# The LRU's gate products taken from high and low parts, in three products instead of one in full precision

## The chip, the cores and the metric

The kernel runs on one core of a Trainium2 chip. The metric is the device time of one execution in microseconds (us), taken as the median of several runs. The engines are named as the profile names them: PE multiplies matrices, PEld loads its weights, DVE and ACT do elementwise work, POOL does little here, and SP issues the transfers between the memory of the device and the core.

## The reference

One layer of a streaming encoder trunk is computed for 512 prompt positions and 8 x 16 sample positions, which makes T = 640 rows of width 1024. After a norm, one wide product with `w_in` feeds three branches: an attention with a forget gate (FoX), a gated linear recurrence (RG-LRU), and gated linear attention (GLA). Their outputs are merged by gates, and an MLP follows. The change touches only the LRU branch:

```python
xc, conv_new = causal_conv(lx, conv_buf, p['lru_conv_w'], p['lru_conv_b'])
hseq, h_last = rg_lru(xc, h0, p['lru_w_a'], p['lru_b_a'], p['lru_w_x'], p['lru_b_x'], p['lru_lambda'])
y_lru = jax.nn.gelu(lg) * hseq.astype(x.dtype)

def rg_lru(x, h0, w_a, b_a, w_x, b_x, lam):
    xb = x.reshape(B, T, LRU_BLOCKS, LRU_BLOCK_DIM)        # 8 blocks of 128 columns
    r = sigmoid(einsum('btni,nij->btnj', xb, w_a) + b_a)   # gate product 1
    i = sigmoid(einsum('btni,nij->btnj', xb, w_x) + b_x)   # gate product 2
    log_a = LRU_C * r * log_sigmoid(lam)
    a = exp(log_a); mult = sqrt(-expm1(2.0 * log_a))
    u = mult * i * x                                       # then h[t] = a[t] * h[t-1] + u[t]
```

## The kernel before, in words

All large products are made from high and low parts. A weight block of 128 output columns (512 KB) is loaded to `w_raw`, ACT casts it to its high part (`hi`, line L1115), DVE subtracts that from the raw block to give the low part (`lo`, line L1541), and PE runs, for each half of the 640 columns and each of 8 slices, three products: high by high, high by low, low by high (`block`, line L584). That is 24 matmuls of 320 columns for a half, 48 for a block. Two sets of buffers alternate, and the two halves have a PSUM bank each (`Z[0]`, `Z[1]`).

The LRU stage works through 8 blocks of 128 channels. The program calls `lru_window(n, ...)` for n = 0 to 8 on every engine; each engine runs its own list of instructions in the order written, and semaphores tie the lists together. Window n does two things at once. For channel block n (`cur`) it computes the two projections: `lx` goes to the tile `XP` (ACT lines L1280, L1299, L1300), is convolved by DVE (L1777 to L1791) into `XC`, and `lg` goes to `LG` (L1120) and into the GELU. For channel block n-1 (`lag`) it makes the gates and the recurrence. The windows 1 to 7 do both; window 0 has only `cur`, window 8 only `lag`. In window n the lists are, in order:

- PE: the first half of the `lx` block, the gate products of block n-1 (`lru_gates`, L790), the second half of the `lx` block, both halves of the `lg` block.
- ACT: copy of the first half of `lx` (L1280), tanh of the GELU (L1285), four tanhs on the gate products (L1290), one more tanh (L1296), copies of the second half of `lx` (L1299, L1300), `hi` of the next window's `lx` block (L1115), exp and square of the decay (L1305, L1306), first half of `lg` (L1120), square root (L1313), second half of `lg` (L1120), square for the GELU (L1318), `hi` of the next window's `lg` block (L1115), and, after DVE's output, the cast to `YH` (L1322).
- DVE: L1762, L1766, `lo` (L1541), L1771 (waits for ACT's L1306), the convolution (it waits for ACT's copies of both halves), L1794, the small fixes L1798 to L1800, the scan over 640 steps (L1801), the output product (L1802, which releases L1322), L1808 (waits for L1318), `lo` (L1541), L1813.
- SP: for window n two weight blocks, and then, when the gate products of the window before are done (`g_mm`), the two 128x128 gate weights into `WG` (L478). A transfer that waits holds all the later ones in SP's list.

The gate products of the kernel before are plain f32 matmuls of `WG` with `XC`, four instructions of 320 columns for each block. The profile shows such an instruction as two records. Their semaphores are `xc_ready` (convolution done), `wg_in` (gate weights arrived) and `r_act` (ACT has read the gates of the block before). Most of the tiles named here are pieces of one large buffer, so that rows call them `arena`.

Of the kernel before, what the change touches and what calls it, by code (L numbers as in the profile page):

```python
# [18 lines left out]
ALU = mybir.AluOpType  # L19
ACT = mybir.ActivationFunctionType  # L20
AX = mybir.AxisListType
F32 = mybir.dt.float32
F32R = mybir.dt.float32r
BF16 = mybir.dt.bfloat16

P = 128
NEG = -1.0e30
ARENA = 22600
# [66 lines left out]
def build(nc, ins, outs):  # L95
# [5 lines left out]
    TP, D = x_prompt.shape[1], x_prompt.shape[2]  # L101
    NB, TS_ = x_sample.shape[0], x_sample.shape[1]
    T = TP + NB * TS_
    HT = T // 2
# [46 lines left out]
    with ExitStack() as ctx:  # L151
# [8 lines left out]
        bank = [psum[:, i, :] for i in range(8)]  # L160
# [33 lines left out]
        arena_at = nc.sbuf_base - 4 * ARENA  # L194
# [20 lines left out]
        A0 = KT * T  # L215
# [6 lines left out]
        def sems(names):  # L222
            return [sem(n) for n in names.split()]
# [23 lines left out]

        wg_in, xc_ready, g_mm, rx_act, r_act, a_act, m_dve, m_act, h_ready, yl_hi, yl_done = sems(
            "wg_in xc_ready g_mm rx_act r_act a_act m_dve m_act h_ready yl_hi yl_done")
        ge_sq, ge_dve, ge_act, ge_out, last_dve, last_pe, last_sb = sems(  # L250
            "ge_sq ge_dve ge_act ge_out last_dve last_pe last_sb")

# [29 lines left out]
        XPW = CONV_W - 1 + TP + NB * (CONV_W - 1 + TS_)  # L282
        (WG, LG, GQ, TG, Y2, RA, RX, AA, TH, A2, MM, UU, HH, XC, XP, LS) = carve(
            A0, (2, P), (T,), (T,), (T,), (T,), (T,), (T,), (T,), (T,), (T,), (T,), (T,), (T,), (T,), (XPW + 1,), (D,))
        XPS = XP[:, CONV_W - 1 + TP:XPW].rearrange("p (b t) -> p b t", b=NB)

        (QG, KG, KTl, ZG, BC, E1, E2, E3, KEM, VT2, VN, QGB, S0, SA, OS, RG, GU, SG) = carve(
            A0, (T,), (T,), (T,), (T,), (T,), (T,), (T,), (T,), (2, P), (2, T), (NT, GLA_DV),
# [69 lines left out]
        def _(sp):  # L358
# [110 lines left out]
            def lru_loads(n, first=False):  # L469
                b = n * 2 + B_LRU  # L470
                c = (lambda c0: n.ds(P, P, c0) if n.terms else slice(c0 + n.c * P, c0 + (n.c + 1) * P))
                load(b, B_LRU % 2, w_in_v[:, :, c(clx)])
                load(b + 1, 1 - B_LRU % 2, w_in_v[:, :, c(clg)])
                if not first:
                    sp.wait_ge(g_mm, n.v)
                nd = n.ds() if n.terms else slice(n.c, n.c + 1)
                for i, w in enumerate((lru_wa, lru_wx)):
                    sp.dma_start(WG[:, i, :], w[0, nd].rearrange("n i j -> (n i) j")).then_inc(wg_in, 16)  # L478
# [93 lines left out]
        def _(pe):  # L572
# [34 lines left out]
            for k in range(KT):  # L607
                mm = pe.transpose(bank[6][:, k * NR:(k + 1) * NR], vrow[0:NR, k * P:(k + 1) * P], idf[0:NR, 0:NR])
# [4 lines left out]
            for r in range(16):  # L613
                mm = pe.transpose(bank[2 + r // 4][0:FOX_HEADS, (r % 4) * P:(r % 4 + 1) * P],
                                  cp_raw[:, r * FOX_HEADS:(r + 1) * FOX_HEADS], idf[:, :])
# [5 lines left out]
            for t in range(NT):  # L621
                mm = pe.transpose(bank[6][:, t * 8:t * 8 + 8], lfT[0:FOX_HEADS, tok(t)], idf[0:FOX_HEADS, 0:FOX_HEADS])
# [3 lines left out]
            for t in range(NT):  # L626
                mm = pe.transpose(bank[7][:, t * 8:t * 8 + 8], cT[0:FOX_HEADS, tok(t)], idf[0:FOX_HEADS, 0:FOX_HEADS])
# [153 lines left out]


            def lru_gates(n):
                pe.wait_ge(xc_ready, (n + 1).v)
                pe.wait_ge(wg_in, (n * 32 + 32).v)
                if n.terms or n.c > 0:
                    pe.wait_ge(r_act, n.v)
                for i in range(2):
                    for h in range(2):
                        mm = pe.matmul(bank[2 + 2 * i + h][:, 0:HT], WG[:, i, :], XC[:, h * HT:(h + 1) * HT],  # L790
                                       start=True, stop=True)
                mm.then_inc(g_mm, 1)

            def lru_window(n, lag):
# [10 lines left out]
            for n in range(LRU_N):  # L805
                mm = pe.transpose(bank[2 + n // 4][0:36, (n % 4) * P:(n % 4 + 1) * P], last[:, n, :], idf[:, :])
# [141 lines left out]
            for c in range(NKC):  # L948
# [3 lines left out]
                for t in range(NT):  # L952
                    mm = rows_block(bank[PAIR[t]], c * KC_W, t, WHW, WLW, b % 2, c == 0, c == NKC - 1)
# [149 lines left out]
        def _(act):  # L1103
            step = Steps(act, act_step)

            def hi(b, s):

                if b.terms or b.c >= 2:
                    act.wait_ge(z_done[1], (b + -1).v)
                hi_to(b, s, WH[s][:, :, :], raw[s][:, :, :])  # L1110
# [158 lines left out]
            def lru_window(n, cur, lag):  # L1269

                b = n * 2 + B_LRU
                s = B_LRU % 2
                m = n + -1
                if not lag:
                    hi(b + 1, 1 - s)
                if cur:
                    if lag:
                        act.wait_ge(xc_ready, n.v)
                    act.wait_ge(z_done[0], (b + 1).v)
                    act.copy(XP[:, 3:3 + HT], Z[0][:, 0:HT]).then_inc(z_free[0], 1)  # L1280
                else:
                    gate(1, Lin(0), b, 0, 0)
                if lag:
                    act.wait_ge(ge_dve, n.v)
                    act.activation(TG[:, :], GQ[:, :], ACT.Tanh, scale=GELU_A).then_inc(ge_act, 1)  # L1285
                    act.wait_ge(g_mm, n.v)
                    act.wait_ge(lru_cols, 1)
                    for dst, bk, r, done in ((RX, 4, R_BX, rx_act), (RA, 2, R_BA, r_act)):
                        for h in range(2):
                            ins_ = act.activation(dst[:, h * HT:(h + 1) * HT], bank[bk + h][:, 0:HT], ACT.Tanh, scale=0.5,  # L1290
                                                  bias=one(col[:, at(m), r:r + 1]))
                        ins_.then_inc(done, 1)
                    act.wait_ge(r_act, n.v)

                    c4, c4n = one(lru_c4[:, 0:1, at(m)]), one(lru_c4[:, 1:2, at(m)])
                    act.activation(TH[:, :], RA[:, :], ACT.Tanh, scale=c4n, bias=c4n)  # L1296
                if cur:
                    act.wait_ge(z_done[1], (b + 1).v)
                    act.copy(XP[:, 3 + HT:3 + TP], Z[1][:, 0:TP - HT])  # L1299
                    act.copy(XPS[:, :, CONV_W - 1:], Z[1][:, TP - HT:HT].rearrange("p (b t) -> p b t", t=TS_)).then_inc(z_free[1], 1)  # L1300
                else:
                    gate(1, Lin(0), b, 0, 1)
                hi(b + 2, s)
                if lag:
                    step(act.activation(AA[:, :], RA[:, :], ACT.Exp, scale=c4, bias=c4))  # L1305
                    act.activation(A2[:, :], AA[:, :], ACT.Square).then_inc(a_act, 1)  # L1306
                if cur:
                    if lag:
                        act.wait_ge(ge_out, n.v)
                    evac(b + 1, 0, LG[:, 0:HT])  # L1310
                if lag:
                    act.wait_ge(m_dve, n.v)
                    act.activation(MM[:, :], MM[:, :], ACT.Sqrt).then_inc(m_act, 1)  # L1313
                if cur:
                    evac(b + 1, 1, LG[:, HT:T])
                    for h in range(2):
                        act.wait_ge(z_free[h], (b + 2).v)
                    act.activation(GQ[:, :], LG[:, :], ACT.Square, scale=GELU_B ** 0.5).then_inc(ge_sq, 1)  # L1318
                    hi(b + 3, 1 - s)
                if lag:  # L1320
                    act.wait_ge(h_ready, n.v)
                    act.copy(YH[:, at(m), :], MM[:, :].unsqueeze(1)).then_inc(yl_hi, 1)  # L1322
# [208 lines left out]
        def _(dve):  # L1531
# [221 lines left out]
            def lru_window(n, cur, lag):  # L1753
# [19 lines left out]
                if cur:  # L1773
# [4 lines left out]
                    for j in range(CONV_W):  # L1778
                        w = one(col[:, at(n), R_CW + j:R_CW + j + 1])
# [12 lines left out]
                if lag:  # L1792
                    dve.wait_ge(m_act, n.v)
                    step(dve.scalar_tensor_tensor(out=UU[:, :], in0=UU[:, :], scalar=0.5, in1=MM[:, :], op0=ALU.mult, op1=ALU.mult))  # L1794

                    h0 = col[:, at(m), R_H0:R_H0 + NB].rearrange("p a b -> p (a b)").unsqueeze(2)
                    first_a, first_u = by_sample(AA)[:, :, 0:1], by_sample(UU)[:, :, 0:1]
                    step(dve.tensor_tensor(fix[:, :, :], first_a, h0, ALU.mult))  # L1798
                    step(dve.tensor_tensor(first_u, first_u, fix[:, :, :], ALU.add))
                    step(dve.memset(first_a, 0.0))  # L1800
                    step(dve.tensor_tensor_scan(HH[:, :], AA[:, :], UU[:, :], 0.0, ALU.mult, ALU.add))  # L1801
                    dve.scalar_tensor_tensor(out=MM[:, :], in0=Y2[:, :], scalar=0.5, in1=HH[:, :], op0=ALU.mult,  # L1802
                                             op1=ALU.mult).then_inc(h_ready, 1)
                    dve.tensor_copy(last[:, at(m), 27:28], HH[:, TP - 1:TP].unsqueeze(1))
                    step(dve.tensor_copy(last[:, at(m), 28:36], by_sample(HH)[:, :, TS_ - 1:TS_].rearrange("p b o -> p o b")))
# [248 lines left out]
```

## Time and profile before

| what | value |
|---|---|
| median of the runs | 1556.79 us |
| lowest and highest of 3 | 1556.17 and 1559.05 us |
| the profiled execution: its own time | 1559.7 us |
| the profiled execution: span of its trace | 1558.0 us |
| granted TensorE clock, mean over the span | 0.989 |
| PE, PEld, DVE, ACT busy | 97%, 90%, 44%, 39% of the span |

The span reaches from the first to the last recorded instruction, and the execution's own time is 1.7 us longer. A granted clock of 1.00 is 2.4 GHz and 0.50 is 1.2 GHz. The busy share of PE is high because matmuls are pipelined and their records overlap; the pitch from one start to the next is a better measure of what a matmul costs in a stream.

### The profile page before, as it was taken

How to read it: one execution, taken by the hardware profiler on the slowest of the kernel's cores; microseconds unless marked ns; L12 is line 12 of the kernel's file. 1: busy time of each engine (PE TensorE's matmuls, PEld its weight loads, DVE VectorE, ACT ScalarE, POOL GpSimd, SP SyncE). 2: the span in 40 equal slices, each digit the busy share in tenths (PEclk: the TensorE clock that was granted, in tenths of full speed). 3: DMA queues.
4: the chain of work that ended last, by engine and by line, in shares of the span. 5: the costliest groups of instructions: out<-in, count | busy, mean ns of one | idle time of the engine just before them, and what ended most of it. 6: DMA issues, size and time to landing. Idle time of an engine off the chain costs nothing.

```text
span 1558.0 us, 25466 instructions
## 1 busy us (share of the span) xinstructions
PE 1509.3 (97%) x9798; PEld 1400.6 (90%) x9798; DVE 692.5 (44%) x1185; ACT 609.4 (39%) x1092; POOL 10.8 (1%) x25
## 2 busy tenths in 40 slices
PE   6999999999999989999999999999899999999997
PEld 6899999989999979998988989987898998998986
DVE  6455555532357872334554543345432323323235
ACT  6233333322157762224554541234441441431532
POOL 1000000000000000000000000000100000000000
PEclk9999999999999999999999999999899999999999
DMA  4645456332313222242332322333022222222221
GB/s 144 162 132 160 123 138 161 83 86 67 85 48 87 61 71 68 67 112 55 113 111 54 112 84 81 99 144 95 28 80 72 78 81 69 80 78 70 82 93 70
DMA packets 224956, 143.50 MB, mean 92 GB/s; under 512 B 7654, under 2 KB 211111, under 8 KB 224892
## 3 DMA queue, kind: packets, MB, share of 16 engines
q1 hardware_dynamic: 224900, 142.72, 31.9%
q8 instruction: 39, 0.64, 0.2%
q14 instruction: 17, 0.14, 0.0%
HBM read 129.86 MB, written 12.84 MB: 92 GB/s over the span
## 4 chain that ended last, share of the span: by engine, by line
PE 84%; DVE 7%; ACT 4%; issue 3%; DMA 2%; DVEq 0%; ACTq 0%; SPq 0%
PE psum L584 57%; PE psum L939 16%; PE psum L691 1%; PE psum L719 1%; PE psum L864 1%; DVE arena L1801 1%; ACT arena L1290 1%; DVE arena L1856 1%; PE psum L702 1%; PE psum L651 1%; PE psum L662 1%; ACT w_hi L1115 1%; PE psum L907 1%; PE psum L905 1%; PE psum L599 1%
## 5 line engine op out<-in xcount | busy, mean ns | idle before, releaser
L584 PE MATMUL psum<-XH,w_hi 128*128 128x320 f32 x1936 | 610.7, 315 | 5.4 <-DVE XL L1547 2.0
L584 PE MATMUL psum<-XH,w_lo 128*128 128x320 f32 x1936 | 600.6, 310 | 0.0
L584 PE MATMUL psum<-XL,w_hi 128*128 128x320 f32 x1936 | 600.6, 310 | 0.0
L1541 DVE TENSOR_TENSOR w_lo<-w_raw,w_hi 128x1024 fp32r<-128x1024 f32 x177 | 216.6, 1224 | 374.7 <-ACT w_hi L1115 374.1
L584 PEld LDWEIGHTS psum<-XH,w_hi 128*128 128x128 f32 x1936 | 365.9, 189 | 18.1 <-issue 7.4
L584 PEld LDWEIGHTS psum<-XL,w_hi 128*128 128x128 f32 x1936 | 366.0, 189 | 0.8
L584 PEld LDWEIGHTS psum<-XH,w_lo 128*128 128x128 f32 x1936 | 365.6, 189 | 0.0
L1115 ACT CAST w_hi<-w_raw 128x1024 fp32r<-128x1024 f32 x177 | 185.3, 1047 | 326.7 <-PE psum L939 155.3
L939 PE MATMUL psum<-w_hi,YH 128*128 128x512 f32 x320 | 125.4, 392 | 2.7 <-DVE YL L1936 2.7
L939 PE MATMUL psum<-w_hi,YL 128*128 128x512 f32 x320 | 125.0, 391 | 0.0
L939 PE MATMUL psum<-w_lo,YH 128*128 128x512 f32 x320 | 125.0, 391 | 0.0
L584 PE MATMUL psum<-YH,w_hi 128*128 128x320 f32 x384 | 119.6, 311 | 1.0 <-DVE YL L1672 1.0
L584 PE MATMUL psum<-YL,w_hi 128*128 128x320 f32 x384 | 119.3, 311 | 0.0
L584 PE MATMUL psum<-YH,w_lo 128*128 128x320 f32 x384 | 119.3, 311 | 0.0
L1970 DVE TENSOR_TENSOR YL<-arena,YH 128x320 f32 (+1 forms) x64 | 31.5, 493 | 148.7 <-ACT YH L1481 148.7
L1120 ACT ACTIVATE arena<-psum 128x320 f32<-128x320 f32 x96 | 41.5, 433 | 101.6 <-PE psum L584 101.4
L939 PEld LDWEIGHTS psum<-w_hi,YH 128*128 128x128 f32 x320 | 60.5, 189 | 15.5 <-issue 3.0
L584 PEld LDWEIGHTS psum<-YH,w_hi 128*128 128x128 f32 x384 | 72.8, 190 | 1.2 <-issue 1.1
L584 PEld LDWEIGHTS psum<-YL,w_hi 128*128 128x128 f32 x384 | 72.7, 189 | 0.0
L584 PEld LDWEIGHTS psum<-YH,w_lo 128*128 128x128 f32 x384 | 72.6, 189 | 0.0
L939 PEld LDWEIGHTS psum<-w_lo,YH 128*128 128x128 f32 x320 | 60.4, 189 | 12.6
L939 PEld LDWEIGHTS psum<-w_hi,YL 128*128 128x128 f32 x320 | 60.5, 189 | 12.4
(249 smaller groups left out, 1420.2 us busy)
## 6 DMA issues: line engine op xcount, KB each, us to landing
w_raw<-in_w_in_dram SPq DMA_DIRECT2D x88, 512.0 KB, 3.9
w_raw<-in_w_up_dram SPq DMA_DIRECT2D x32, 512.0 KB, 4.0
w_raw<-in_w_down_dram SPq DMA_DIRECT2D x32, 512.0 KB, 3.5
w_raw<-in_w_branch_dram SPq DMA_DIRECT2D x24, 512.0 KB, 3.9
arena<-in_cache_fox_k_dram SPq DMA_DIRECT2D x8, 1024.0 KB
arena<-in_cache_fox_v_dram SPq DMA_DIRECT2D x8, 1024.0 KB
out_dram<-arena SPq DMA_DIRECT2D x16, 256.0 KB, 2.4
arena<-in_state_gla_dram SPq DMA_DIRECT2D x4, 1024.0 KB, 5.4
```

Source lines behind the costliest of these rows:

```text
L584: mm = pe.matmul(Z[h][:, 0:HT], w[s][:, k, :], x[:, k, h * HT:(h + 1) * HT], start=(k == 0 and i == 0), stop=(k == KT - 1 and i == 2))
L599: mm = pe.transpose(bk[:, k * P:(k + 1) * P], HS[:, t % 2, (4 * q + k) * P:(4 * q + k + 1) * P], idf[:, :])
L651: mm = pe.transpose(TBK[j % 2][:, i * P:(i + 1) * P], KC[par][:, 4 * j + i, :], idf[:, :])
L662: mm = pe.transpose(TBK[j % 2][:, (i - 4 * j) * P:(i - 4 * j + 1) * P], src[:, par, tok(i % NT)], idf[:, :])
L691: pe.matmul(S[:, 0:w], QT[:, par, tok(t)], KTt[:, par, 0:w], start=True, stop=False)
L702: mm = pe.transpose(TBK[2][:, i * P:(i + 1) * P], SP[:, p % 2, i * P:(i + 1) * P], idf[:, :])
L719: mm = pe.matmul(O[:, 0:P], KVN[:, i, :], pt[:, i * P:(i + 1) * P], start=(i == 0), stop=(i == t))
L939: mm = pe.matmul(O[:, 0:HD], x[:, k0 + k, tok(t)], w[c][:, k, :], start=(first and k == 0 and i == 0), stop=(last and k == KC_W - 1 and i ...
L1115: act.copy(dst, src).then_inc(w_hi, 1)
L1120: act.activation(dst, Z[h][:, 0:HT], ACT.Copy, scale=scale).then_inc(z_free[h], 1)
L1541: dve.tensor_tensor(dst, src, h.bitcast(F32), ALU.subtract).then_inc(w_lo, 1)
L1970: dve.tensor_tensor(YL[:, bass.ds(j, 1), half], UQ[:, half].unsqueeze(1), YH[:, bass.ds(j, 1), half].bitcast(F32), ALU.subtract).then_inc( ...
```

## The change

The gate products are made the same way as the large ones. ACT casts the gate weights `WG` (256 columns) to `WGH` and the convolution output `XC` (640 columns) to `XGH`; DVE subtracts to get `WGL` and `XGL`; PE runs 12 matmuls of the fp32r type for a block instead of 4 of type f32. The two casts stand on ACT after L1318 and ahead of the `hi` of the next `lg` block. The two subtractions stand on DVE between L1794 and L1798. In window n they belong to channel block n, and PE uses them in window n+1. SP loads new gate weights when DVE's second subtraction is done (`xg_lo_done`), and no longer when the gate products are done. The four new tiles lie behind those of the stage in the same buffer.

```diff
 (SP, lru_loads)
                 if not first:
-                    sp.wait_ge(g_mm, n.v)
+                    sp.wait_ge(xg_lo_done, n.v)
                 ...
 (PE)
             def lru_gates(n):
-                pe.wait_ge(xc_ready, (n + 1).v)
-                pe.wait_ge(wg_in, (n * 32 + 32).v)
+                pe.wait_ge(xg_hi_done, (n + 1).v)
                 if n.terms or n.c > 0:
                     pe.wait_ge(r_act, n.v)
-                for i in range(2):
-                    for h in range(2):
-                        mm = pe.matmul(bank[2 + 2 * i + h][:, 0:HT], WG[:, i, :], XC[:, h * HT:(h + 1) * HT],
-                                       start=True, stop=True)
+                for j, (w, x) in enumerate(((WGH, XGH), (WGH, XGL), (WGL, XGH))):
+                    if j == 1:
+                        pe.wait_ge(xg_lo_done, (n + 1).v)
+                    for i in range(2):
+                        for h in range(2):
+                            mm = pe.matmul(bank[2 + 2 * i + h][:, 0:HT], w[:, i, :], x[:, h * HT:(h + 1) * HT],
+                                           start=(j == 0), stop=(j == 2))
                 mm.then_inc(g_mm, 1)
 (ACT, lru_window)
                     act.activation(GQ[:, :], LG[:, :], ACT.Square, scale=GELU_B ** 0.5).then_inc(ge_sq, 1)
+                    act.wait_ge(wg_in, (n * 32 + 32).v)
+                    act.copy(WGH[:, :, :], WG[:, :, :])
+                    act.wait_ge(xc_ready, (n + 1).v)
+                    act.copy(XGH[:, :], XC[:, :]).then_inc(xg_hi_done, 1)
                     hi(b + 3, 1 - s)
 (DVE, lru_window)
                 if lag:
                     dve.wait_ge(m_act, n.v)
                     step(dve.scalar_tensor_tensor(out=UU[:, :], in0=UU[:, :], scalar=0.5, in1=MM[:, :], op0=ALU.mult, op1=ALU.mult))
+                if cur:
+                    dve.wait_ge(xg_hi_done, (n + 1).v)
+                    dve.tensor_tensor(WGL[:, :, :], WG[:, :, :], WGH[:, :, :].bitcast(F32), ALU.subtract)
+                    dve.tensor_tensor(XGL[:, :], XC[:, :], XGH[:, :].bitcast(F32), ALU.subtract).then_inc(xg_lo_done, 1)
+                if lag:
                     h0 = col[:, at(m), R_H0:R_H0 + NB].rearrange("p a b -> p (a b)").unsqueeze(2)
```

The lines of the changed kernel are numbered higher, by 7 to 17 in the rows that follow. First the list of DVE in the body of the loop over the windows 1 to 7, from the end of the convolution to the scan. Before:

```order
L1791 COPY last<-arena 128x24
L1794 SCALAR_TENSOR_TENSOR arena<-arena 128x640
L83 REGISTER_ALU
L1798 ISA
L1798 TENSOR_TENSOR fix<-arena,col 128x8
```

And with the change, at the same place:

```order
L1804 COPY last<-arena 128x24
L1807 SCALAR_TENSOR_TENSOR arena<-arena 128x640
L83 REGISTER_ALU
L1809 REGISTER_ALU
L1810 TENSOR_TENSOR wg_lo<-arena,wg_hi 128x256
L1811 TENSOR_TENSOR xg_lo<-arena,xg_hi 128x640
L1815 ISA
L1815 TENSOR_TENSOR fix<-arena,col 128x8
```

The two subtractions came in ahead of the fixes, and so ahead of the scan and of the output product behind them. Next ACT's list from the copy of the second half of `lg` to the cast to `YH`, before:

```order
L1120 ACTIVATE arena<-psum 128x320
L1318 ACTIVATE arena<-arena 128x640
L1114 REGISTER_ALU
L1115 CAST w_hi<-w_raw 128x1024
L1322 ISA
L1322 COPY YH<-arena 128x640
```

And with the change:

```order
L1129 ACTIVATE arena<-psum 128x320
L1327 ACTIVATE arena<-arena 128x640
L1328 ISA
L1329 CAST wg_hi<-arena 128x256
L1330 REGISTER_ALU
L1331 CAST xg_hi<-arena 128x640
L1123 REGISTER_ALU
L1124 CAST w_hi<-w_raw 128x1024
L1335 ISA
L1335 COPY YH<-arena 128x640
```

The two casts stand between the GELU's square and the weight block's high part. The cast of the weight block now follows a wait for the convolution.

## Rows read from the trace of the kernel before

**Rows 1.** The page: the chain that ended last, shares by engine.

```profile
PE 84%; DVE 7%; ACT 4%; issue 3%; DMA 2%; DVEq 0%; ACTq 0%; SPq 0%
```

**Rows 2.** Chain that ended last, 425 to 590 us: start, us, what.

```profile
462.00 0.18 DVE fix L1798
...
496.50 0.18 DVE fix L1798
...
502.63 1.68 ACT arena L1290 x4
...
507.53 0.75 ACT arena L1306
...
513.75 0.18 DVE fix L1798
...
565.50 0.18 DVE fix L1798
```

**Rows 3.** Timeline of ACT, 494 to 520 us; in brackets the idle time before.

```profile
510.55 0.42 ACT L1120 ACTIVATE arena<-psum 128x320 f32<-128x320 f32 x1
511.06 0.74 ACT L1318 ACTIVATE arena<-arena 128x640 f32<-128x640 f32 x1
...
516.77 0.73 ACT L1322 CAST YH<-arena 128x640 f32 x1 [4.03 <-DVE arena L1802]
```

**Rows 4.** Timeline of DVE, 494 to 520 us.

```profile
512.69 0.17 DVE L1791 COPY last<-arena 128x24 f32 x1
512.77 0.82 DVE L1794 SCALAR_TENSOR_TENSOR arena<-arena 128x640 f32<-128x640 f32 x1
...
515.82 0.82 DVE L1802 SCALAR_TENSOR_TENSOR arena<-arena 128x640 f32<-128x640 f32 x1
...
517.65 1.22 DVE L1541 TENSOR_TENSOR w_lo<-w_raw,w_hi 128x1024 fp32r<-128x1024 f32 x1
518.79 0.82 DVE L1813 TENSOR_TENSOR YL<-arena,YH 128x640 f32 x1
```

**Rows 5.** Timeline of PE, 444 to 449 us: gate products between two halves.

```profile
443.82 0.31 PE L584 MATMUL psum<-XH,w_lo 128*128 128x320 f32 x1
...
446.17 2.31 PE L790 MATMUL psum<-arena 128*128 128x320 f32 x8
...
448.46 0.31 PE L584 MATMUL psum<-XL,w_hi 128*128 128x320 f32 x1
```

**Rows 6.** Timelines of ACT, then of SP, windows 0 and 1, 426 to 470 us.

```profile
443.38 0.74 ACT L1318 ACTIVATE arena<-arena 128x640 f32<-128x640 f32 x1
...
448.65 1.78 ACT L1290 ACTIVATE arena<-psum,col 128x320 f32<-128x320 f32 x4 [1.22 <-PE psum L790]
...
452.04 0.32 ACT L1299 COPY arena<-psum 128x192 f32<-128x192 f32 x1 [0.54 <-PE psum L584]
...
453.88 1.05 ACT L1115 CAST w_hi<-w_raw 128x1024 fp32r<-128x1024 f32 x1 [1.35 <-DMA w_raw<-in_w_in_dram]
...
459.07 0.44 ACT L1120 ACTIVATE arena<-psum 128x320 f32<-128x320 f32 x1 [0.18 <-PE psum L584]
...
448.65 0.35 SPq L478 DMA_DIRECT2D arena<-in_lru_w_a_dram  x1
...
450.02 1.02 SPq L363 DMA_DIRECT2D w_raw<-in_w_in_dram  x2
```

**Rows 7.** Timeline of PE: the first matmuls behind two long pauses.

```profile
42.61 0.47 PE L622 MATMUL psum<-ident,arena 8*128 8x8 f32 x5 [1.90 <-DVE arena L1601]
...
584.80 1.87 PE L806 MATMUL psum<-ident,last 128*36 128x128 f32 x8 [6.38 <-DVE fix L1821]
```

**Rows 8.** Stretches: us, busy PE, PEld, DVE, ACT, POOL, PEclk, DMA share, GB/s.

```profile
42.00:48.00 6.00, 5.39 (x28) 5.37 (x29) 4.40 (x7) 0.00 (x0) 0.00 (x0) 0.72 0.12 15
52.00:54.00 2.00, 0.93 (x9) 0.84 (x8) 1.33 (x2) 1.63 (x3) 0.00 (x0) 1.00 0.05 14
582.00:590.00 8.00, 5.20 (x22) 4.83 (x23) 3.12 (x7) 4.72 (x6) 0.00 (x0) 0.57 0.00 0
```

More of the change, by code:

```diff
@@ L249, in build @@
             "wg_in xc_ready g_mm rx_act r_act a_act m_dve m_act h_ready yl_hi yl_done")
+        xg_hi_done, xg_lo_done = sems("xg_hi_done xg_lo_done")
         ge_sq, ge_dve, ge_act, ge_out, last_dve, last_pe, last_sb = sems(
@@ L285, in build @@
         XPS = XP[:, CONV_W - 1 + TP:XPW].rearrange("p (b t) -> p b t", b=NB)
+        A_LG = -(-(A0 + 2 * P + 13 * T + XPW + 1 + D) // 8) * 8
+        XGH, XGL = (nc.alloc_sbuf_tensor_at(name, [P, T], F32R, offset=arena_at + 4 * (A_LG + i * T))
+                    for i, name in enumerate(("xg_hi", "xg_lo")))
+        WGH, WGL = (nc.alloc_sbuf_tensor_at(name, [P, 2, P], F32R, offset=arena_at + 4 * (A_LG + 2 * T + i * 2 * P))
+                    for i, name in enumerate(("wg_hi", "wg_lo")))
+        assert A_LG + 2 * T + 4 * P <= ARENA
         (QG, KG, KTl, ZG, BC, E1, E2, E3, KEM, VT2, VN, QGB, S0, SA, OS, RG, GU, SG) = carve(
```

## The prediction

> **What bounds the kernel now.** First I read the page's chain by engine: 84% of it is PE [rows 1], so one would expect any cheaper matmul to help. That is a mean over stages, so next I read the chain in the stretch that is changed, the LRU stage at about 425 to 590 us. There the chain hardly touches PE. It goes round once in each window: the fixes, scan and output product on DVE, then ACT's list with L1290 and L1306 in it, then DVE's convolution, L1794 and the fixes again [rows 2]. The same instruction, L1798, stands at 496.50 and at 513.75, so a turn is 17.25 us; from the first at 462.00 to the last shown at 565.50 there are six turns, and 103.50 / 6 is 17.25 too. ACT waits 4.03 us for DVE before L1322 [rows 3], and DVE waits for ACT elsewhere: the two pass one thread to and fro.
>
> Then I read what PE needs for a window. Sixteen starts from 443.82 to 446.17 give a pitch of 0.147 us for a matmul of 320 columns [rows 5]. The gate products begin at 446.17, and the second matmul behind them at 448.46, so that the first stood at 448.31 by the pitch: 2.14 us for the four f32 instructions. With 96 matmuls in two blocks PE needs 96 x 0.147 + 2.14 = 16.25 us in a turn of 17.25. PE idles 1.0 us in each turn, and the loop over ACT and DVE sets the pace.
>
> **What PE gains.** Twelve fp32r matmuls at that pitch take 1.76 us, 0.38 less than the 2.14. PE's need falls to 15.9 us. In the steady windows this is worth nothing, since PE already waits there; if PE did set the pace, it would be 8 x 0.38 = 3.0 us.
>
> **What ACT and DVE have to do more.** The trace of before has no cast or subtraction of 256 columns. For 640 columns a cast took 0.73 us (L1322) [rows 3] and one for 1024 columns 1.05 [rows 6], so a line through both gives 0.41 for 256. A subtraction took 0.82 for 640 columns (L1813) and 1.22 for 1024 (L1541) [rows 4], so 0.42 for 256. Bounds: not under nothing, not over the 0.73 and 0.82 of the wider ones; I take the lines, since the size lies near and the kind of work is the same. Back-to-back instructions overlap by 0.08 (L1791 starts at 512.69, lasts 0.17, and L1794 starts at 512.77; it has 0.09 there) [rows 4].
>
> **Where it stands in the loop.** In the frame of the turn that ends at 513.75:
> - ACT ends the copies and the square L1318 at 511.80 [rows 3]. The cast of the gate weights fits behind it, to 512.1, in a time in which ACT idled later. It costs nothing, covered by the 4.03 us.
> - The convolution is done at 512.69 + 0.17 = 512.86 [rows 4]. ACT picks such a signal up 0.13 later (L1802 ends at 515.82 + 0.82 = 516.64 [rows 4], L1322 starts at 516.77 [rows 3]) and casts 640 columns: 512.99 to 513.72.
> - DVE does L1794 meanwhile (512.77 to 513.59) and then waits for that cast. Its first subtraction starts at 513.76, almost exactly when L1798 started before. So the wait itself costs nothing over the 0.16 that DVE lost there anyway, and the subtractions cost all: (0.42 - 0.08) + (0.82 - 0.08) = 1.08. L1798 starts at 514.84 instead of 513.75: **1.09 us later**.
> - Behind it on DVE are queued the fixes, the scan, the output product, and for the product ACT waits with L1322; ACT's table load and L1280 follow at once, then all of the turn. Nothing in the turn has slack to take it up. A turn becomes 18.34 us.
>
> What is late next: the cast of the next `lg` block now follows the cast of `XC`, so it ends near 514.8 instead of 512.75. Its subtraction stood at 517.65 behind DVE's output product [rows 4] and moves on by 1.09 too, so it does not see this. On PE the first four gate matmuls wait for the cast, the other eight for the subtraction, and the second half of `lx` stands behind them. They end 8 x 0.147 = 1.2 us after the subtraction, that is about 1.3 us after L1798; ACT's L1290 wants them 502.63 - 496.50 = 6.1 us after it [rows 2]. The second half of `lx` is done 3.5 us later, at 4.8, and ACT wants it when L1290 has ended, at 7.8. PE has room. On SP the gate weights no longer wait for the gate products but for the second subtraction, which is earlier, and two weight loads stand behind them in the list; in the steady windows no cast waits for a load, so this brings nothing there.
>
> **Windows 0 and 1.** Window 0 has no recurrence on DVE, so its subtractions delay nothing: L1318 at 443.38 [rows 6], casts to 445.1, subtractions to 446.3, while PE reaches the gates at 446.17 and needs the low parts only at 446.76. Here PE and SP count. The gate products end 0.38 us earlier, so L1299, which waited for PE, goes from 452.04 to 451.66 [rows 6]. The gate weights are issued at 446.45 instead of 448.65, so the next weight load goes from 450.02 to 447.82 and lands by 451.7; its cast then follows L1299 after 0.35, at 452.0 instead of 453.88. That gives 1.87 us to the thread, and the convolution of window 1 ends at 459.24 instead of 461.11. But ACT cannot use all of it: its copy of the second half of `lg` waits for PE, and moves only from 459.07 to 458.69. Then come L1318 (0.51 behind, as in [rows 3]) at 459.20, the two casts from 459.84 to 460.9, and the two subtractions: L1798 at 462.03, against 462.00 before. So window 1 costs nothing: the gain of 1.87 pays for its 1.09 and for ACT's late casts.
>
> **Sum.** Windows 2 to 7 are six turns of 1.09 = 6.5 us, and with the 0.03 of window 1 it is +6.6 us. Window 8 has neither casts nor subtractions. The stages before and after are bound by PE as they were; they just begin later. Against the profiled execution's own 1559.7 us that gives 1566.3; that execution lies 2.9 us above the median, and I put the same 6.6 us on the median: **1563.4 us**, 0.42% slower. The case's own range: with the window 1 paying its 1.09 in full (its gain lost elsewhere) 7.6 us, and with no overlap at DVE (1.24 a turn, seven turns) 8.7; with a 256-column subtraction that costs nothing 6 x 0.74 = 4.4. So 1561.2 to 1565.5.
>
> **Rivals.**
> - *The work is hidden.* DVE is busy 44% of the span, so 1.1 us of it could vanish in idle time. If the thread did not run through L1798, only the gain of windows 0 and 1 would be left: 0 to -1.9 us, 1554.9 to 1556.8. Against it: DVE runs its list in order, the scan is in the thread in all seven turns, and the 0.16 us ahead of L1798 is its only slack [rows 2, 4]. Chance 0.08.
> - *PE sets the pace, and the kernel gets faster.* The price is 3.0 us for the eight gate products, and the 1.87 us of window 1 with it: 1551.9, 0.3% faster. This decides only if the turn over ACT and DVE is shorter than PE's 15.9 us; it reads 17.25 and grows. Chance 0.04.
> - *The clock falls.* TensorE's clock is at its full level of 2.4 GHz in this stage, to judge by the pitch of 0.147 us [rows 5]. With the change PE idles 18.34 - 15.9 = 2.4 us in a turn, about 1.0 ahead of the gates, 0.6 between their parts, the rest before the first half of `lg`. Behind a pause of 1.90 us [rows 7] the stretch 42 to 48 had 0.72 of the clock [rows 8], a loss of 6 x 0.28 = 1.7 us of work; behind 6.38 us of pause [rows 7] the stretch 582 to 590 had 0.57 [rows 8], a loss of 3.4 us. On the other side, in 52 to 54 us PE was busy only 0.93 us of 2 and kept the full clock [rows 8]. A loss of 1.7 in each turn PE could take from its idle 2.4; one of 3.4 would put at most 1.0 more on each of six or seven turns, another 6 to 7 us: 1569 to 1570. Chance 0.08. The Trainium skill (TensorE: Matmul & The Clock Gate, Part 1) says that the throttled clock is the default and that activity releases it, which speaks for this rival; by that rule, every pause of the new kind is a risk that the kernel before did not run. The two pauses above agree with it, and the stretch at 52 us shows that a short one may pass.
>
> **Chances and range.** Forecast 0.80, hidden 0.08, faster by PE 0.04, clock 0.08. A measurement of this kernel tells about 0.2% (3.1 us) from no change. Faster by over 0.2%: 0.04. Within: 0.09, the hidden case and a thin edge of the forecast. Slower: 0.87. The range takes the forecast's 1561.2 to 1565.5, widened by some 0.7 us below and 2 us above, for the spread of the runs (2.9 us between lowest and highest) and for a clock that falls in a few turns: 1560.5 to 1567.5.
>
> **What the changed profile would show.** Right: the fixes behind the subtractions (L1815 there) repeat every 18.3 us; the first of them stands near 462.0; the subtractions last 0.42 and 0.82 us and the first starts right as the cast ends; PE idle ahead of and between the gate matmuls grows, with 0.147 us from one of them to the next; L1322's successor still waits for DVE. Wrong would be a period near 17.25 (hidden), a period under it (PE), PE's matmuls at a pitch of 0.27 us in the stage (clock), or a first turn that comes later than 462. What would upset the sum most is a cast of `XC` that starts well behind the end of the convolution, since DVE stands behind it and every tenth of a microsecond counts six times.

## The result and the profile after

| | before | with the change |
|---|---|---|
| median of 6 executions each | 1556.64 us | 1566.51 us |
| lowest and highest | 1555.77 and 1560.25 | 1565.76 and 1568.20 |
| profiled execution, own time / span | 1559.7 / 1558.0 | 1567.08 / 1564.4 |
| ratio of the times | | 1.0061 (95% interval 1.0050 to 1.0071) |

The kernel is slower by 0.61%. The forecast was slower by 0.42%, 1563.4 us in a range of 1560.5 to 1567.5. So the sign and the range held and the size is some 3 us short. The two spans differ by only 6.4 us, though the medians differ by 9.9; that gap is the question of what follows. A ratio is estimated over the executions and need not be the quotient of the two medians.

The chain that ended last in the changed kernel, in the LRU stage: start, duration, what. The scan is L1818 here and stands 0.54 us behind the first fix.

```profile
462.75 1.50 DVE arena L1818
...
572.43 1.50 DVE arena L1818
```

Six turns take 572.43 - 462.75 = 109.68 us, 18.28 each, against 17.25 in [rows 2]. The next rows are of its ACT, then of its DVE, in the turn that ends at 517 us. They answer to [rows 3] and [rows 4].

```profile
513.97 0.39 ACT L1329 CAST wg_hi<-arena 128x256 fp32r<-128x256 f32 x1
515.15 0.72 ACT L1331 CAST xg_hi<-arena 128x640 fp32r<-128x640 f32 x1 [0.79 <-DVE last L1804]
```

```profile
515.03 0.82 DVE L1807 SCALAR_TENSOR_TENSOR arena<-arena 128x640 f32<-128x640 f32 x1
515.97 0.43 DVE L1810 TENSOR_TENSOR wg_lo<-arena,wg_hi 128x256 fp32r<-128x256 f32 x1
516.31 0.82 DVE L1811 TENSOR_TENSOR xg_lo<-arena,xg_hi 128x640 fp32r<-128x640 f32 x1
517.05 0.16 DVE L1815 TENSOR_TENSOR fix<-arena,col 128x8 f32<-128x8 f32 x1
```

The first cast fits behind the square and leaves ACT 0.79 us idle before the second, so the first cast is free. The first fix starts 517.05 - 515.03 = 2.02 us behind L1807; before it was 513.75 - 512.77 = 0.98 [rows 2, 4]. The turn is 1.04 us longer at just this place. PE, in the same turn:

```profile
515.93 0.85 PE L799 MATMUL psum<-xg_hi,wg_hi 128*128 128x320 f32 x4 [0.57 <-ACT xg_hi L1331]
517.19 0.85 PE L799 MATMUL psum<-xg_lo,wg_hi 128*128 128x320 f32 x4 [0.41 <-DVE xg_lo L1811]
```

Its new waits for the parts are there, 0.57 and 0.41 us, and nobody waits for PE in turn. In windows 0 and 1, SP issues the first gate weights (L485) at 446.62 us, where [rows 6] have 448.65. Two rows of ACT there answer to [rows 6] as well:

```profile
452.23 1.06 ACT L1124 CAST w_hi<-w_raw 128x1024 fp32r<-128x1024 f32 x1
...
458.90 0.44 ACT L1129 ACTIVATE arena<-psum 128x320 f32<-128x320 f32 x1 [1.03 <-PE psum L591]
```

The gate weights are issued 2.0 us earlier, the cast of window 1 no longer waits for its load (452.23 for 453.88), and ACT then waits for PE at 458.90.

To see where the rest comes from I compared when ACT casts each weight block. At the entry of the stage the changed kernel is 0.23 us late (L1327 at 443.61, L1318 at 443.38). At the first cast behind the stage it is 6.39 late (L1124 at 594.00, L1115 at 587.61). So the stage costs 6.2 us. All other differences lie at three places where PE pauses: right behind the stage (6.4 us), ahead of the out projection near 1031 us (2.7 us), and near 1100 us (3.6 and 1.4 us). The stretch of 20 us around the pause ahead of the out projection, first in the kernel before, then in the changed one (columns as in [rows 8]; PEclk is the third from the end):

```profile
1025.00:1045.00 20.00, 17.26 (x85) 14.97 (x84) 11.53 (x16) 7.18 (x11) 0.00 (x0) 0.91 0.15 53
```

```profile
1030.00:1050.00 20.00, 17.26 (x81) 14.96 (x80) 11.19 (x16) 7.41 (x11) 0.00 (x0) 0.83 0.15 53
```

Both pause for the same 2.7 us, and both have a fallen clock behind it (1.2 GHz for a part of the stretch), the changed kernel for longer.

### The profile page after: what moved, and what is told of

The parts are those of the page before. It is cut to its first block, busy times and chain, and to the rows that moved or that the text cites. A ratio compares the mean times of both kernels' runs of the same rounds, so it can differ in the third digit from the quotient of the medians.

```text
span 1564.4 us, 25576 instructions
## 1 busy us (share of the span) xinstructions
PE 1506.7 (96%) x9830; PEld 1400.7 (90%) x9830; DVE 701.2 (45%) x1201; ACT 617.5 (39%) x1108; POOL 10.8 (1%) x25
## 4 chain that ended last, share of the span: by engine, by line
PE 84%; DVE 7%; ACT 4%; issue 3%; DMA 1%; DVEq 0%; ACTq 0%; SPq 0%
PE psum L591 58%; PE psum L948 16%; PE psum L698 1%; PE psum L726 1%; PE psum L873 1%; DVE arena L1818 1%; ACT arena L1299 1%; DVE arena L1873 1%; PE psum L709 1%; PE psum L658 1%; PE psum L669 1%; PE psum L916 1%; PE psum L914 1%; ACT w_hi L1124 1%; PE psum L606 1%
## 5 line engine op out<-in xcount | busy, mean ns | idle before, releaser
L1124 ACT CAST w_hi<-w_raw 128x1024 fp32r<-128x1024 f32 x177 | 185.4, 1047 | 325.1 <-PE psum L948 156.6
```

What stands on the lines that cost most here:

```text
L1124: act.copy(dst, src).then_inc(w_hi, 1)
```

## Experiments

Each job also timed the kernel before on the same chip; ratios are against those.

**e1, the kernel before once more.** No edit.

> The kernel before, unchanged, for a second trace and more times. The two traces differ by 6.4 us of span, the medians by 9.9. Theory A (the profiled execution of before was one of its slower ones, by some 3 us of clock falls and start-up waits, and the true difference is about 9.5): most executions here have spans near 1555 us, median 1556.5. Theory B (the medians differ by luck and the true difference is the 6.2 us that the LRU stage shows): the span is near 1558 again and the median near 1559. In both the turn of the LRU stage is 17.25 us.

Median of 12: 1556.85 us (1555.74 to 1559.63); beside it 23 executions of the same program had 1558.91 (1555.19 to 1561.85). The ratio is 0.9996 (0.9986 to 1.0006). The turn is 17.26 us. The span of the profiled one is 1554.0 us, as theory A wants, but the times form two groups: of the 12 spans seven are 1554.0 to 1555.4 at a mean clock of 0.990 to 0.993, and five are 1557.3 to 1557.9 at 0.989 to 0.990. The other 23 spread from 1553.5 to 1560.1 and their order follows the clock: up to 1555.0 at 0.992 to 0.993, from 1555.4 to 1557.5 at 0.989 to 0.990, from 1558.4 on at 0.987 to 0.988. Executions with times near the lowest, at a clock of 0.992 or more, are called the low group below, and all others the upper. By that cut six of e1's 12 are low, and the 1555.4 at 0.990 stands between the groups. The same stretch as above, of this execution of the kernel before:

```profile
1025.00:1045.00 20.00, 17.26 (x89) 14.92 (x89) 10.63 (x15) 7.12 (x10) 0.00 (x0) 1.00 0.22 75
```

The same program, the same pause, and here the clock stays full. At the pause right behind the stage the two traces of the kernel before differ as well. First the first trace, then e1's:

```profile
588.00:590.00 2.00, 2.00 (x9) 2.00 (x9) 1.22 (x1) 0.65 (x1) 0.00 (x0) 0.55 0.00 0
```

```profile
588.00:590.00 2.00, 2.00 (x15) 2.00 (x15) 1.23 (x1) 0.74 (x1) 0.00 (x0) 1.00 0.00 0
```

The clock came back 2 us later in the first trace, which cost it 1.0 us. The first trace of before was thus one of the upper group, and so was the changed kernel's: their 6.4 us compare like with like.

**e6, the changed kernel once more.** No edit.

> The changed kernel, unchanged, beside more executions of the kernel before. The kernel before has shown two groups of times, near 1556.2 at a mean clock of 0.993 and near 1559 at 0.989, which part behind the LRU stage and at the pause of the out projection near 1031 us; the changed kernel's six were all at a clock of 0.988 to 0.991. Theory A (the stage costs 6.3 us, and the rest of the 9.5 is which of those groups the executions fell into): over more executions the changed kernel shows a group near 1562.5 too, and the ratio of the medians comes down towards 1.004 to 1.005. Theory B (the shift by 6 us puts the later pauses at a bad place each time): all executions at 1565 or more, ratio 1.005 to 1.006.

Median of 6: 1566.46 us (1562.38 to 1567.79), ratio 1.0059 (1.0045 to 1.0072). One of the six is in a low group of its own, with a span of 1560.7 us; the other five are at 1563.9 to 1565.9. The profile is of the low one:

```profile
1030.00:1050.00 20.00, 17.26 (x92) 15.16 (x91) 11.84 (x16) 7.51 (x11) 0.00 (x0) 1.00 0.18 55
```

Against e1's trace it is 1560.7 - 1554.0 = 6.7 us longer, and in both the clock holds at this pause. Of the 6.7 us, 6.0 arise in the LRU stage; the rest arises at the other two pauses, where both lose clock (the table behind e11). The result lies between the theories: the low group exists, as A said, but the ratio did not come down, as B said. Over both jobs 1 of 12 executions of the changed kernel was in the low group. Of the kernel before it was 10 of 23 in this job, and 23 of 63 over the three jobs of this section, e1's own 12 left out.

**e2, casts and subtractions, but the old products.**

```diff
+ (SP) sp.wait_ge(g_mm, n.v)                 # besides xg_lo_done
- (PE) 12 matmuls of WGH, WGL with XGH, XGL, and the waits for xg_hi_done, xg_lo_done
+ (PE) the waits for xc_ready and wg_in, as before
+ (PE) pe.matmul(bank[2 + 2 * i + h][:, 0:HT], WG[:, i, :], XC[:, h * HT:(h + 1) * HT], start=True, stop=True)
```

> The changed kernel, with its casts and subtractions in their places, but with the gate products of the kernel before (four f32 matmuls for a block, from WG and XC). The new parts are made and not used. Thread theory (the subtractions on DVE lengthen the turn over ACT and DVE, and PE's gain is worth nothing): turn 18.3 us as in the changed kernel, median 1566.5 to 1568, the last us for the gate weights, which wait for the products again in window 0. Rival (PE has a part in the loop, by its waits for the parts): turn nearer to 17.6, median under 1563.

The new parts are computed and not used. Median of 6: 1564.70 us, ratio 1.0041 (1.0026 to 1.0057). From the chain:

```profile
464.12 1.50 DVE arena L1817
...
573.80 1.50 DVE arena L1817
```

These are the first and the last of seven, so a turn is 18.28 us, the same to a hundredth as with the new products. Which of the two products PE computes has no part in the turn. The first scan comes 1.4 us later than in the changed kernel: 0.1 us because this trace entered the stage later, and the rest is the gain of windows 0 and 1 that went. The expected median, 1566.5 to 1568, was missed: it is 1.8 us under the changed kernel's. In this trace the clock held at the out projection's pause (1.00 from 1025 to 1045 us, span 1561.5 at a mean clock of 0.993), and three of the six executions had a mean of 0.993.

**e3, the casts alone.**

```diff
- (DVE) both subtractions
- (PE)  12 matmuls, 4 f32 ones of WG and XC as before
+ (SP) sp.wait_ge(xg_hi_done, n.v); sp.wait_ge(g_mm, n.v)
```

> Only the two casts on ACT are added to the kernel before; no subtraction, f32 products from WG and XC. Thread theory: the casts lie in time in which ACT waits anyway, turn 17.25 us, median as before (1556 to 1557.5). Rival (the longer list of ACT or its wait for the convolution costs too): turn 17.6 to 18, median 1559 to 1562.

The output is the kernel before's; the casts' results are not read. Median of 12: 1558.48, ratio 0.9999 (0.9989 to 1.0009). The median is above the 1557.5 that I allowed, but the kernel before had 1558.91 beside it. Scans at 462.10 and 565.65 give 17.26 us a turn. The casts are free.

**e7, one subtraction more.**

```diff
+ dve.tensor_tensor(XGS[:, :], XC[:, :], XGH[:, :].bitcast(F32), ALU.subtract)   # spare tile, not read
  dve.tensor_tensor(XGL[:, :], XC[:, :], XGH[:, :].bitcast(F32), ALU.subtract).then_inc(xg_lo_done, 1)
```

> The changed kernel with one more subtraction of 640 columns on DVE at the same place, its result not used. Thread theory: each us on DVE between L1794 and the fixes counts fully, so a turn grows by 0.82 - 0.08 = 0.74 us, from 18.28 to 19.02, and the median by 6 to 7 turns of it, 4.4 to 5.2 us over the changed kernel of this job. Rival (DVE has slack there and the 1.03 us of a turn come from the wait for ACT's cast): turn 18.3 to 18.6.

Median of 5: 1572.31 us, 5.85 over e6 in the same job. From the chain:

```profile
463.87 1.50 DVE arena L1820
...
578.00 1.50 DVE arena L1820
```

From the first to the last of seven a turn is 19.02 us, 0.74 more, as expected to a hundredth. The 5.85 us of the median are above the expected 4.4 to 5.2. DVE has no slack at this place.

**e10 and e11, the two pauses filled,** in the kernel before and in the changed one.

```diff
+            for _ in range(38):       # ahead of the transposes behind the LRU stage
+                pe.matmul(bank[6][:, 0:HT], XH[:, 0, 0:P], XH[:, 1, 0:HT], start=True, stop=True)
             pe.wait_ge(r_act, LRU_N)
             pe.wait_ge(last_dve, 1)
...
+            for _ in range(16):       # ahead of the out projection
+                pe.matmul(bank[3][:, 0:HT], XH[:, 0, 0:P], XH[:, 1, 0:HT], start=True, stop=True)
```

> The kernel before, with matmuls whose results nobody reads in two pauses of PE: 38 of 320 columns ahead of the wait in front of L806, and 16 ahead of the wait in front of the out projection. They fit into the pauses (5.6 of 6.4 us, 2.4 of 2.7). Clock theory (the two groups of times are clock falls behind those pauses): the granted clock stays full there, the spread within the kernel shrinks to about 1 us, and the median falls by 1 to 4 us, to 1553 to 1556. Rival (the groups come from elsewhere, as transfers): spread and median as before.

> The changed kernel with the same matmuls in the same two pauses. Theory A (stage cost plus clock luck): the difference to the kernel before with filled pauses is the stage's alone, 6.0 to 6.6 us. Theory B (the change costs another 3 us outside of the stage that is not the clock): the difference stays at 9 to 10 us.

e10: median of 12 1556.44 us (1555.32 to 1560.18), ratio 1.0000 (0.9989 to 1.0010). e11: median of 12 1560.98 us (1560.32 to 1564.23), ratio 1.0021 (1.0012 to 1.0031). The stretch behind the LRU stage, in e10, and the one at the out projection, in e11:

```profile
578.00:594.00 16.00, 15.19 (x107) 14.88 (x106) 7.57 (x16) 6.97 (x9) 0.00 (x0) 1.00 0.23 67
```

```profile
1030.00:1050.00 20.00, 19.61 (x103) 17.19 (x102) 11.21 (x15) 7.13 (x10) 0.00 (x0) 1.00 0.24 79
```

With matmuls in them the two pauses no longer cost clock; the first had 0.79 over its 16 us in the two unfilled traces of either kernel (584 to 600 us in the changed one). The changed kernel gained 1566.46 - 1560.98 = 5.5 us by it. The kernel before shows no gain beyond its noise: its median is 2.0 us under that of the unfilled executions beside it, but e1's, without any edit, was 2.1 under those beside it, and the ratio is 1.0000. The difference of the two medians is 4.5 us, where e6 had 8.0 in the same job. Theory A said 6.0 to 6.6 and B 9 to 10: B is out, and 4.5 lies 1.5 under A. The spread of e10 did not shrink to 1 us as I expected: three of its 12 are still at spans of 1558.0 to 1558.4 at a clock of 0.991. The pause near 1100 us was not filled.

The traces say where the time went. The table has the start of the same cast of a weight block on ACT, in us, for e1, and for the other five traces how much later it starts there:

| cast | e1 | before | changed | e6 | e10 | e11 |
|---|---|---|---|---|---|---|
| ahead of the stage | 414.99 | 0.03 | 0.26 | -0.10 | 0.00 | -0.43 |
| last of the stage | 574.56 | -0.08 | 6.30 | 5.92 | -0.01 | 5.67 |
| behind the first pause | 594.32 | 0.89 | 6.86 | 6.20 | -1.34 | 4.35 |
| ahead of the out projection | 1016.41 | 0.90 | 6.88 | 6.22 | -1.32 | 4.37 |
| behind the out projection's pause | 1046.77 | 2.37 | 9.72 | 6.22 | -1.32 | 4.34 |
| behind the pauses near 1100 us | 1145.31 | 3.95 | 10.38 | 6.63 | -0.40 | 4.92 |

Behind 415 us the casts move against each other only in the stage and at the three pauses. The stage costs 6.2, 6.0 and 6.1 us in the three pairs (changed and before, e6 and e1, e11 and e10). The traces of the filled pair differ by only 5.4 us because e11 had entered the stage 0.4 us earlier and because e10 lost 0.9 us against e1 at the unfilled pauses near 1100 us where e11 lost 0.6. At the first pause the fill gained 1.3 us against e1 for the kernel before and 1.6 against e6 for the changed one. At the out projection's pause the clock held in e1 and e6 too, so there was nothing to gain against them; against the first traces it is 1.5 and 2.8 us.

**e4, the subtractions behind the output product** (L1815, L1817, L1818 there), all else as in the change.

> The changed kernel with the two subtractions moved on DVE from ahead of the fixes to behind the output product and the two copies after it. Thread theory: the thread over ACT and DVE is back at 17.25 us, but the gate products now end about 5.4 us behind the fixes, with the second half of lx behind them, done near 8.95, and ACT wants it at 8.8 after the fixes: turn 17.3 to 17.7, median 1556 to 1559.5. Rival (the cost of the change is not the subtractions' place but their work or PE's waits): turn near 18.3, median near 1566.

Median of 6: 1565.87 us, ratio 1.0050 (1.0034 to 1.0067): no gain. Scans at 460.23 and 572.72 give 18.75 a turn, and they alternate between 18 and 19.5 us. My expectation missed here. Two of its stretches:

```profile
484.00:487.00 3.00, 3.00 (x15) 3.00 (x14) 2.13 (x3) 2.60 (x5) 0.00 (x0) 0.60 0.84 225
```

```profile
502.00:505.00 3.00, 3.00 (x23) 3.00 (x22) 2.97 (x5) 2.90 (x7) 0.00 (x0) 1.00 0.42 96
```

PE now pauses 1.9 us ahead of the second part of the gate products, with the second half of `lx` behind it. In one turn the clock falls behind the pause (0.60), in the next it holds (1.00), though the two pauses are alike (1.87 and 1.86 us). That is the forecast's clock rival, in a variant whose pause is longer than the changed kernel's 0.57 and 0.41. ACT then waits for PE at L1308, 1.79 us in the slow turn and 0.51 in the other, so that PE is in the thread in both.

**e5, and the gate products behind the second half of `lx` as well.**

```diff
-                block(b, B_LRU % 2, XH, XL, ((lambda: lru_gates(n + -1)) if lag else None, None))
+                block(b, B_LRU % 2, XH, XL, (None, (lambda: lru_gates(n + -1)) if lag else None))
                 ...
-            merge_begin(1, (lambda: lru_gates(Lin(LRU_N - 1)), None))
+            merge_begin(1, (None, lambda: lru_gates(Lin(LRU_N - 1))))
```

> The changed kernel with the two subtractions behind the output product (as in e4) and the gate products on PE behind the second half of lx, no longer between the halves. Thread theory: the thread over ACT and DVE is as in the kernel before; the subtractions end 4.2 us behind the fixes, the gate products 5.4 behind them, ACT's tanhs want them at 6.0, and no half of a block waits behind them. Turn 17.25 us, median within 0.1% of the kernel before. Rival (e4's long turns came from the work itself): turn 18 or more.

Median of 5: 1565.64 us, ratio 1.0048 (1.0036 to 1.0061): missed again. Scans at 464.92 and 572.75, 17.97 a turn. First two rows of the chain, between which SP issues the gate weights (at 505.06), then one of ACT's timeline:

```profile
504.08 0.83 DVE xg_lo L1822
...
506.42 3.92 DMA w_raw<-in_w_in_dram
```

```profile
510.36 1.05 ACT L1124 CAST w_hi<-w_raw 128x1024 fp32r<-128x1024 f32 x1 [0.56 <-DMA w_raw<-in_w_in_dram]
```

SP's gate weights wait for the subtraction, which comes late now, and the next weight block's load stands behind them in SP's list. Its cast on ACT waits 0.56 us for it, and that cast is in the thread: scan, output, subtraction, SP, load, cast, L1314, convolution, scan. The subtractions left one thread and came back in by another. That another order of SP's list, with the weight load first, would mend this was not tried.

**e8, the kernel before with the convolution first.**

```diff
-                lo(b + 2, s)
-                if lag:
-                    (L1771: MM from A2 and TH)
                 if cur:
                     ...
                     for j in range(CONV_W):
                         ...
+                        if j == 0:
+                            lo(b + 2, s)
+                        if j == 1:
+                            (L1771, if lag)
```

> The kernel before with DVE's order changed in a window: the convolution starts as soon as ACT has copied lx, with lo of the next block behind its first three instructions and L1771 behind its first five; before, the convolution stood behind both. Nothing is added or left out. Thread theory: the thread falls to about 15.6 us, under PE's 16.25, so that PE sets the pace: turn 16.25 to 16.5, median 5 to 7 us under the kernel before. Rival (a turn is bound by something else, as ACT's whole list): turn 17 to 17.3.

Median of 5: 1550.86 us (1548.62 to 1553.56), ratio 0.9949 (0.9935 to 0.9963): 0.5% faster than the kernel before, the best of all. The median is 7.8 us under the kernel before's in its job, where 5 to 7 were expected. Scans at 462.47 and 560.31, 16.31 us a turn, PE's 16.25 almost exactly. The stage:

```profile
440.00:570.00 130.00, 130.00 (x835) 124.91 (x834) 102.78 (x195) 100.68 (x155) 0.00 (x0) 1.00 0.28 72
```

PE is busy the whole of it. The thread over ACT and DVE was the bound, and shortening it by order alone gives what the change could not.

**e9, the new products with e5's and e8's orders; e12, e9 with the fill.**

> e5 with the order of e8: gate products from high and low parts, subtractions behind the output product, gate products behind both halves of lx, convolution first. Thread theory: PE now sets the pace with 15.85 us of work, and here the 0.38 us that the fp32r products save are worth their price: turn 15.9 to 16.2, 0.2 to 0.4 under e8's, median 1 to 3 us under e8's. Rival (waits on PE for the parts eat the 0.38): turn as in e8 or longer.

> e9 with the matmuls of e10 and e11 in the two pauses of PE behind the LRU stage and ahead of the out projection. Clock theory: fewer executions in the slow group, median 0 to 3 us under e9's. Rival (the fill delays what stands behind it, since the pauses are shorter now): median the same or above.

e9: median of 12 1556.09 us, ratio 0.9994 (0.9984 to 1.0004), scans at 463.85 and 564.17, 16.72 a turn, with the same 0.56 us wait of the cast for its load. The 0.38 us of PE is not collected, and e9 is 5.2 us above e8. The rival had the time right and the reason not: over six turns PE's matmuls wait 0.2 us in all for the parts of the gate products and 2.6 us for the low parts of a weight block, and the chain runs by SP's load and the cast, as in e5. e12: median of 5 1552.33 us, ratio 0.9965 (0.9952 to 0.9978), 3.8 under e9, a little more than the 0 to 3 expected. Its fill pays; it does not reach e8.

## Why the prediction was right, and where its size was off

- *The thread over ACT and DVE sets the pace, PE does not.* Right, and shown: e2 keeps PE's old work and has the same 18.28 us, e8 shortens the thread alone and falls to PE's own 16.3.
- *The casts are free, the subtractions cost their whole length.* Right: e3 turns in 17.26, e7 adds exactly 0.74. The cast of 256 columns took 0.39 (0.41 forecast), the subtraction 0.43 (0.42).
- *1.09 us a turn.* It measured 1.03. The term was 0.06 too large: the subtractions cost the 1.08 forecast, but ACT picked the convolution's signal up 0.03 us behind its end (515.12 to 515.15) and not 0.13, and DVE picked up the cast 0.10 behind its end and not 0.04.
- *Window 1 costs nothing.* Nearly: the fixes of window 1 came at 462.21 for 462.03, 0.18 later, which is the 0.23 of the stage's entry. e2, without the earlier gate products and loads, has its first scan 1.4 us later, 1.2 without the later entry, which shows that this gain is real.
- *The stage: +6.6 us.* It measured 6.2, 6.0 and 6.1 in three pairs of traces, close to six turns of 1.03.
- *"The stages before and after are bound by PE as they were; they just begin later."* This is the step that failed, and with it the size. The stages behind have pauses of 6.4, 2.7, 3.6 and 1.4 us behind which TensorE's clock falls for longer in some executions than in others. The two traces of the unchanged kernel differ by 4.0 us, and all of it arises at these pauses: 1.0, 1.5 and 1.6 us. Like with like, the two kernels differ by 6.4 us of span in the upper group (first traces) and 6.7 in the low one (e6, e1), to either side of the forecast's 6.6, and 6.2 and 6.0 of it arise in the stage. What the result has beyond that is which group the executions fell in: 1 of 12 of the changed kernel's were in the low group and 23 of 63 of the kernel before's. The Trainium skill (TensorE: Matmul & The Clock Gate, Part 1) says that the chip's watch over activity runs freely and does not start anew with a kernel, so that the same kernel can differ from run to run. These traces agree: over 20 us at the out projection's pause the kernel before had 0.91 and 1.00, the changed kernel 0.83 and 1.00. That a program moved by 6 us meets it more often at a bad moment fits, and is argued, not shown; by the share of 23 in 63, twelve executions would hold at most one of the low group in about one case of 30, so that luck is not quite excluded.
- *The base.* Part of the 9.9 us is luck of the draw. Four of the six executions of the kernel before in the result have times of the low group (1555.8 to 1556.8), and their median is 1556.64. The executions beside the later runs had medians of 1558.91, 1558.45 and 1558.68, and e6 in its job is 8.0 us over the kernel before.
- *The clock rival* was priced in the wrong place. In the stage the changed kernel kept 1.00 (440 to 575 us), and its pauses there were 0.57 and 0.41 us. It came true in e4 with a pause of 1.9 us, and outside of the stage. Its 3.4 us of loss were too many: of the stretch 582 to 590 us, 2.8 us lie ahead of the first matmul at 584.80 [rows 7, 8], in which a low clock costs nothing.
- *Hidden work* and *PE sets the pace* did not come about.
- *The profiled execution against the median.* I noted that it lay 2.9 us above and took it for a constant offset. It was one execution of the upper group, with clock falls that those of the low group do not have.

What stays open is the last 0.9 us between the 5.4 by which the filled pair's traces differ and the 4.5 of their medians, and whether the changed kernel would stay in the upper group on another placement of its pauses. No run moved a pause without changing anything else.

## What to carry to other kernels

Before making matmuls cheaper, look whether the stage's turn is as long as PE's own work; here a turn of 17.25 us over 16.25 of PE said that the thread over ACT and DVE sets the pace, and a new instruction in it cost its full length (0.74 us in e7) while the casts beside it cost nothing (e3). When two kernels are some microseconds apart, compare traces that lost the same at the pauses, or many executions with the clock beside each. If the thread is the bound, look at the order of its instructions first: starting the convolution 3 us earlier gave 0.5% with no instruction saved. When work is moved out of one thread, follow every semaphore it raises, SP's too: the transfer behind it can carry it back in.

## What the runs showed of the hardware that I had not expected

- Behind the same pause of 2.7 us the granted clock was 1.00, 0.91 or 0.83 over 20 us, in executions of the same or nearly the same program. From the last weight cast ahead of it to the first casts behind, the changed kernel's first trace lost 2.8 us against e1's at this pause. Such losses split e1's 12 times of an unchanged kernel into two groups 3 us apart. Matmuls without a reader held the clock at 1.00 in the two pauses and took 5.5 us off the changed kernel's median and 3.8 off e9's; for the kernel before the times show no gain, and its upper group stayed.
- With pauses of 0.4 to 0.6 us in each turn of 18.3 the clock stayed at 1.00 (440 to 575 us, the changed kernel and e6); behind pauses of 1.9 us in e4 it fell in every second turn.
